# Moving tiles cut at column 256: out tiles and mLSTM projections in token parts of 256 and 320 columns

## Time and profile before

| | us |
|---|---|
| median of three executions | 1880.62 (1880.25 to 1882.64) |
| the profiled execution | 1879.91 |
| its span, first to last instruction | 1878.1 |
| PE busy in the span | 1855.2 (99%) |
| DVE, ACT, POOL busy | 1251.5, 866.9, 329.5 |

### The profile page before, as it was taken

The page is one execution under the profiler, slowest core; times in us unless marked ns, Lnnn a source line. Parts: engine busy times, 40 slices in busy tenths (PEclk is TensorE's granted clock), DMA queues, the critical chain, the costliest instruction groups (busy, mean ns, idle before and its releaser), DMA issues.

```text
span 1878.1 us, 34441 instructions
## 1 busy us (share of the span) xinstructions
PE 1855.2 (99%) x13850; PEld 1834.6 (98%) x13850; DVE 1251.5 (67%) x1999; ACT 866.9 (46%) x1518; POOL 329.5 (18%) x352
## 2 busy tenths in 40 slices
PE   8999999999999999999999999999999999999998
PEld 8999999998999999999999999999989999999998
DVE  7874487668884488679853886563546888548853
ACT  7552355347552355346532553232334665235532
POOL 2220122131220122132201221300010322012112
PEclk9999999999999999999999999999999999999999
DMA  8773576334763576347644763231113576357632
GB/s 207 166 149 105 128 167 148 108 85 95 166 147 108 127 167 150 107 107 165 146 131 102 171 141 101 86 102 68 57 45 103 117 169 152 108 120 167 135 93 82
DMA packets 116830, 234.71 MB, mean 125 GB/s; under 512 B 13184, under 2 KB 15248, under 8 KB 116672
## 3 DMA queue, kind: packets, MB, share of 16 engines
q1 hardware_dynamic: 77440, 160.59, 28.7%
q0 software_dynamic: 38208, 69.42, 22.5%
q10 hardware_dynamic: 1024, 2.49, 0.4%
HBM read 228.92 MB, written 3.53 MB: 124 GB/s over the span
## 4 chain that ended last, share of the span: by engine, by line
PE 93%; DVE 4%; ACT 2%; DMA 1%; issue 1%; DVEq 0%; ACTq 0%
PE ps L1850 49%; PE ps L1840 39%; DVE w_lo L1231 1%; PE ps L1895 1%; PE ps L2167 1%; PE ps L2233 0%; DVE u L1285 0%; DMA raw_z<-in_ffn_in 0%; PE ps L2170 0%; DMA x<-in_x 0%; PE ps L2032 0%; PE ps L2157 0%; DVE rstd L1302 0%; ACT w_hi L726 0%; PE ps L2142 0%
## 5 line engine op out<-in xcount | busy, mean ns | idle before, releaser
L1850 PE MATMUL ps<-u,w_hi 128*128 128x288 f32 x4928 | 984.0, 295 | 11.7 <-DVE w_lo L1231 4.5
L1850 PEld LDWEIGHTS ps<-u,w_hi 128*128 128x128 f32 x4928 | 790.6, 188 | 16.4 <-DVE w_lo L1231 9.4
L1850 PE MATMUL ps<-u,w_lo 128*128 128x288 f32 x2464 | 727.1, 295 | 0.0
L1850 PEld LDWEIGHTS ps<-u,w_lo 128*128 128x128 f32 x2464 | 462.6, 188 | 0.0
L1840 PE MATMUL ps<-h_hi,w_hi 128*128 128x288 f32 x1386 | 294.4, 293 | 0.0
L1840 PE MATMUL ps<-h_lo,w_hi 128*128 128x288 f32 x1386 | 294.3, 293 | 0.0
L1840 PE MATMUL ps<-h_hi,w_lo 128*128 128x288 f32 x1386 | 294.3, 293 | 0.0
L726 ACT ACTIVATE w_hi<-w_raw 128x768 fp32r<-128x768 f32 (+3 forms) x164 | 136.0, 836 | 316.6 <-PE ps L1840 240.2
L1231 DVE TENSOR_TENSOR w_lo<-w_raw,w_hi 128x768 fp32r<-128x768 f32 (+3 forms) x164 | 168.8, 1038 | 160.6 <-ACT w_hi L726 158.4
L1840 PEld LDWEIGHTS ps<-h_hi,w_lo 128*128 128x128 f32 x1386 | 220.4, 188 | 0.0
L1840 PEld LDWEIGHTS ps<-h_hi,w_hi 128*128 128x128 f32 x1386 | 220.3, 188 | 0.0
(11 more groups left out here) (268 smaller groups left out, 2123.5 us busy)
## 6 DMA issues: line engine op xcount, KB each, us to landing
raw_a<-in_ffn_in SPq DMA_DIRECT2D x132, 256.0 KB, 4.2
w_raw<-in_ffn_out SPq DMA_DIRECT2D x64, 384.0 KB, 3.2
raw_y<-in_ffn_in SPq DMA_DIRECT2D x88, 256.0 KB, 3.6
raw_x<-in_ffn_in SPq DMA_DIRECT2D x88, 256.0 KB, 2.7
raw_x<-in_ffn_in POOLq DMA_DIRECT2D x88, 256.0 KB, 6.5
raw_y<-in_ffn_in POOLq DMA_DIRECT2D x88, 256.0 KB, 4.9
raw_z<-in_ffn_in POOLq DMA_DIRECT2D x88, 256.0 KB, 5.1
w_raw<-in_ffn_out SPq DMA_DIRECT2D x64, 320.0 KB, 3.0
```

Of the source, the lines that this page charges most:

```text
L1850: mm = pe.matmul(dst, w, m, start=prod in ("M1", "M2", "M5") and kp == 0 and p == 0, stop=kp == KP - 1 and p == 2, skip_group_check=prod i ...
```

## The change

Both token parts of every `block_mm` begin at the residue of the weights. The parts are columns 0 to 255 and 256 to 575 (`CUT = 256`), 1024 and 1280 bytes long. The regions `hall` and `um` move by 128 bytes, so that their rows begin at residue 128. The two parts are written to columns 256 to 511 of the first bank and columns 0 to 319 of the next, so that they are one run of 576 floats over the border of the banks, and DVE reads them as such (`whole`) instead of as two runs (`pair`). The number of matmuls, weight loads and columns is the same.

```diff
+CUT = 256
-    um_at = u_at + KP * 2 * 7 * HALF * 4 - 2 * DT * TOK * 4
+    um_at = u_at + KP * 2 * 7 * HALF * 4 - 2 * DT * TOK * 4 + 128
...
+    align(256, 128)
     hall = region(2 * PAIRS * TOK * 4)
...
+    def whole(b):
+        return ps[:, b:b + 2, :].rearrange("p b n -> p (b n)")[:, CUT:CUT + TOK]
+
+    def cut(b, h):
+        return ps[:, b, CUT:2 * CUT] if h == 0 else ps[:, b + 1, 0:TOK - CUT]
...
-                return dve.tensor_tensor(halves(dst), pair(bank), halves(rstd[:, :]), ALU.mult)
+                return dve.tensor_tensor(dst, whole(bank), rstd[:, :], ALU.mult)
...
-                    dve.tensor_tensor(halves(x[:, j, :]), halves(x[:, j, :]), pair(out_bank(j)), ALU.add) \
+                    dve.tensor_tensor(x[:, j, :], x[:, j, :], whole(out_bank(j)), ALU.add) \
                         .then_inc(x_ready if ph else x_part, 1)
...
-            dve.scalar_tensor_tensor(halves(q_t[:, 0, :]), pair(2), float(P) ** -0.5,
-                                     halves(rstd[:, :]), ALU.mult, ALU.mult).then_inc(proj_read, 1)
+            dve.scalar_tensor_tensor(q_t[:, 0, :], whole(2), float(P) ** -0.5,
+                                     rstd[:, :], ALU.mult, ALU.mult).then_inc(proj_read, 1)
...
-                    for h in range(2):
-                        mm = pe.matmul(ps[:, bank + h, 0:HALF], w, m[:, h * HALF:(h + 1) * HALF],
-                                       start=first and p == 0, stop=last and p == 2)
+                    for h, at in enumerate((slice(0, CUT), slice(CUT, TOK))):
+                        mm = pe.matmul(cut(bank, h), w, m[:, at], start=first and p == 0, stop=last and p == 2)
```

More of the change, by code:

```diff
@@ L1583, in _ @@
                 if 1 < g <= 4:
-                    dve.scalar_tensor_tensor(halves(q_t[:, g - 1, :]), pair(b), float(P) ** -0.5,
-                                             halves(rstd[:, :]), ALU.mult, ALU.mult).then_inc(proj_read, 1)
+                    dve.scalar_tensor_tensor(q_t[:, g - 1, :], whole(b), float(P) ** -0.5,
+                                             rstd[:, :], ALU.mult, ALU.mult).then_inc(proj_read, 1)
                 elif g > 4:
@@ L1751, in _ @@
                 dve.wait_ge(unit_used, U_MOUT + j + 1)
-                dve.tensor_tensor(halves(x[:, j, :]), halves(x[:, j, :]),
-                                  pair(out_bank(j) if j >= 2 else 2 * j), ALU.add).then_inc(x_ready, 1)
+                dve.tensor_tensor(x[:, j, :], x[:, j, :], whole(out_bank(j) if j >= 2 else 2 * j), ALU.add) \
+                    .then_inc(x_ready, 1)
                 if j < DT - 1:
```

## The result

The changed kernel is slower: 1889.47 us median against 1882.64 for the kernel before (seven runs each), a ratio of 1.0037 with a 95% interval of 1.0026 to 1.0048. The forecast of 1872 had the wrong sign. 1889 lies inside the range, and near where the third rival, the upper level everywhere, put it (1891).

A forecast was written before the change was run, and what follows sets the result against it. PE's back-to-back matmuls bound the kernel. Out phases (-3.5) and mLSTM (-4.8) gave -8.3 us: 1879.9 to 1871.6, plus 0.7 for the median 1872.3, said as 1872; range 1853 to 1892 (own range 1868 to 1877).

The forecast's parts named there:

- third rival: Out phases at 130.0 ns a matmul go to the upper level, 133.3: +10.3 us, 1891; chance 0.28.
- What bounds the kernel: Whole kernel: PE busy 99% of the span; only the distance between matmul starts counts, not supply or eviction.
- residue step: Changed matmuls: both parts starting at the weights' residue makes a pair cost 260.0 ns, 130.0 a matmul on average.
- Prices of single parts: Block matmuls: rows can't price one part alone, since the timeline rounds to 10 ns; they give 260.0 or 266.7 a pair.
- first rival: Out phases and mLSTM: aligned starts give a shorter level, about 126.7 ns a matmul, worth 27 us: 1853; chance 0.21.
- The sum: Two out phases at 133.3 ns gain 3.5 us, the mLSTM 4.8, the other out phases nothing: -8.3 us.
- second rival: Changed matmuls: nothing happens; excess isn't due to addresses, the level depends on how a phase is entered: 1877 to 1883; chance 0.17.
- The weight load as the one cause: At full clock, only the weight load beside each matmul can take the 10 to 13.3 ns beyond its stream.
- The Trainium skill's two ports: TensorE reads moving data and weights through independent ports; by that no residue could matter and the change is worth nothing.
- DVE and the product tiles: Adds stay at 753 ns, costed at nothing; product tiles stay at 132.2 ns, taken as 0, possibly 5.9 us either way.

The follow-up runs named there:

- e1: Kernel of streams alone: 60 fp32r matmuls each, one width (256 to 512 columns) at one moving-minus-weights address distance, then alternating pairs, in two turns; no kernel time given.
- e3: Kernel before with the regions of h and um moved by 128 bytes, half 0 at the weights' residue, half 1 off it: 1878.81 us, 0.9982.
- e11: The changed kernel repeated word for word, one execution: 1886.94 us.
- e5: Streams alone, 36 matmuls each: 176 combinations of distances for pairs and triples, and weight loads of 32, 64 and 96 columns; no kernel time given.
- e6: Streams alone, 48 matmuls each: 88 combinations of cut of 576 columns and distance, plus five triples, three times in three orders; no kernel time given.
- e8: Changed kernel with the cut at 264 and the out tiles' parts at distances 96 and 128 from the weights: 1875.03 us, 0.9969 of the kernel before.
- e2: Changed kernel with the regions of h and um back at residue 0, both parts 128 bytes off the weights: 1876.3 us, 0.9973 of the kernel before.
- e10: The kernel before repeated word for word, another single execution: 1881.16 us.
- e9: Changed kernel with the cut at 272 and the region of h at distance 64 from the weights: 1890.22 us, 1.0046 of the kernel before.
- e7: Changed kernel with only the cut changed, 264 instead of 256: 1869.93 us, 0.9946 of the kernel before.

## Why the prediction was wrong, point by point

**What bounds the kernel**: right. PE does, the waits on DVE at line 1840 didn't change, and 10.3 of the 11.6 us lie in the distance between the matmul starts of the out phases.

**The residue step is the one that failed.** It took 260.0 ns for the new pair, "since phases hold fixed levels, and 260.0 is the nearest one seen". Measured: 266.7, the other level seen. The rows gave both and nothing in them chose; I chose by the sum of two middle rows, 118.4 + 143.3. The first was right to 1 ns (117.5). The second was 149.2: that term was 5.9 ns too small. Of the 6.7 ns by which 260.0 missed, 5.0 are the sum's (5.9 less 0.9) and 1.7 came from taking the seen level below it. The assumption behind it, that 320 has the excess over the stream that 288 has at the lower level, rested on no row: e1 has 320 alone at 13.3 over its stream, and in alternation with 256 at distance 0 it stands 15.9 over it in the changed kernel.

**Prices of single parts would not have helped.** The prediction says that the rows can't give one of the two parts its own price. The starts in the trace do: in the phases at 130.0 of the kernel before, the part off the weights' residue stands at 132 ns and the part on it at 128, and in e3, where the addresses are swapped, so are these two. By that the change should have gained. In that kernel's phases at 133.3 the distances repeat over four matmuls, 131, 131, 132 and 140. A level is the mean of such a repeating sequence of a pair, not the sum of two prices. The distance of 126 that the first rival took for a sign is one matmul at the edge of a phase.

**The sum** followed from the residue step: -3.5 for two phases and -4.8 for the mLSTM became 0 and 0, and the phases at 130.0, costed at no change, gave +10.3 us in the profiled executions. The third rival had exactly this price, 3102 matmuls x 3.33 ns.

**Its reason was half right.** That the two reads never change their relation when all parts are alike fits e1 and e11, where 256 and 320 at distance 0 have one level, but e5 and e6 have no rule of that kind: (264 at 96) is at one level too in its three turns and in e8, and it is the lower. That the part of 256 lacks slack is wrong: e2 has the same parts and goes at 130.0 in five phases, and 272, with more slack, is worse.

**The 10.3 us in the profile are 6.8 in the medians.** I read one profiled execution of the kernel before as its normal state. e10 shows another, with seven slow out phases instead of two and faster product phases. The second rival's sentence, that which level a phase takes depends on how it is entered, fits the kernel before, whose phases change level between executions at the same addresses (that it is the entry that picks isn't shown), and not the changed one, whose sixteen phases in two executions have one level.

**The weight load as the one cause** of what a matmul costs beyond its stream is not shown: with a load a quarter as long 6.7 to 10.0 ns of 13.3 are left (e5).

**The Trainium skill's two ports.** e1 has 256 columns with one and the same load at 120.0 and at 113.3 ns, where only the start of the moving tile differs, and e5 has them at 113.3 instead of 120.0 at distance 0 when only the load is shorter. That speaks against the sentence of the Trainium skill, "TensorE: Matmul & The Clock Gate", step 1 of "Step-by-step: what each phase is for", that loading the next weights doesn't take read bandwidth from the running matmul, for fp32r at least. If the two reads never met, their distance should not matter; where they meet is not shown.

**DVE and the product tiles**: 753 ns as forecast; the products stayed on their two levels.

**Open**: what the two reads share. The two levels of the out phases differ by 6.67 ns a pair (260.0, 266.7), which at twice the rate of the earlier trace rows is the time of 16 columns or 64 bytes; but other combinations settle elsewhere (264.4, 268.9 and 273.3 a pair), so that is an observation on these two and not a rule. Also open is what picks the level of a phase, at its entry or elsewhere.

## What to carry to other kernels

In a kernel bound by back-to-back matmuls, the distance between two starts can hold one of a few levels for a whole phase, and addresses and widths select which ones there are; read it from the chain (length over count) for each phase, and for more than one execution, before putting a price on it. When two levels are on record and no row chooses, a stream of 50 matmuls with nothing else running narrows it down for a few microseconds of chip time: it reproduced the changed kernel's level and forecast those of e8 and e9. It has to be run in several turns, and even three missed the second level of e7. A symmetrical arrangement isn't a safe one: it can be locked in the worse level.

## What the runs showed of the hardware

- fp32r matmuls of 320 columns with a weight load of 128 cost 146.7 ns at every distance; 512 columns at distance 0 cost 226.7, at 128 some 232. At distance 0 the excess over the stream is 12 to 13 ns for all five widths from 256 to 512; at 128 it is 12 ns for 256 and 19 for 512 (e1).
- 256 columns cost 113.3 ns alone at distance 192, yet 118 between matmuls of 320 at the same distance (131.7 on average; e1): a price measured in a uniform stream doesn't carry over to a mixed one.
- Of the 88 combinations of cut and distance in e6 none settled lower than 260 ns for the 576 columns in any turn; six have that price in all three, among them the cut at 264 at two distances (0 and 96).
- Levels differ from one execution to the next (two of eight out phases slow, then seven of eight); 24 timed executions of the kernel before lie between 1877.36 and 1888.42 us. The changed kernel, with one level in all its profiled out phases, still ranges from 1885.22 to 1891.49, so levels of the out phases aren't all of the spread.
